# Three edits to a one-core, five-layer block: state-space coefficients loaded and computed first, step sizes cut in four, and a bias table copied 16 times instead of 128

## What is computed

```python
# first block: an input projection, a causal convolution, softplus step sizes, a chunked scan
h = rms_norm(x, norm_g[l]);  proj = h @ w_in[l]
xbc = jax.nn.silu(causal_dwconv(xbc, ssd_conv_w[l], ssd_conv_b[l]))
dt = jax.nn.softplus((dt_raw + ssd_dt_bias[l]).astype(jnp.float32))
y = ssd_scan(xs, dt, -jnp.exp(ssd_a_log[l]), bs, cs)
# second block, layer 0 (s5_mixer): coefficients from parameters alone
dt = jnp.exp(log_dt)[:, None];  mag = jnp.exp(lr * dt)
ab_re, ab_im = mag * jnp.cos(li * dt), mag * jnp.sin(li * dt)
den = lr * lr + li * li;  nr = ab_re - 1.0
f_re = (nr * lr + ab_im * li) / den;  f_im = (ab_im * lr - nr * li) / den
# second block, layer 1 (sliding_window_attention): a bias by distance, added to the scores
dist = qi + WINDOW - kj
bias = rel_bias[t5_bucket(jnp.maximum(dist, 0))]
s = jnp.where(valid, s + bias, NEG_INF)
```

## Time and profile before

| | us |
|---|---|
| median of three runs | 2254.06 (2251.0 to 2259.76) |
| the profiled execution's own time | 2256.19 |
| its span | 2254.4 |
| TensorE busy | 2045.3 (91%) |
| VectorE busy | 1289.9 (57%) |
| ScalarE busy | 872.2 (39%) |
| GpSimd busy | 477.9 (21%) |
| mean granted TensorE clock | 0.959 |

### The profile page before, as it was taken

How to read it: one execution, slowest core, us unless ns; L and a number is a source line. 1 busy time by engine, 2 the same in 40 slices (tenths; PEclk the granted TensorE clock), 3 DMA queues, 4 the chain that set the end, 5 groups by cost and what they waited for, 6 DMA issues and landing times.

```text
span 2254.4 us, 25022 instructions
## 1 busy us (share of the span) xinstructions
PE 2045.3 (91%) x10070; PEld 1593.4 (71%) x10070; DVE 1289.9 (57%) x1830; ACT 872.2 (39%) x1263; POOL 477.9 (21%) x386
## 2 busy tenths in 40 slices
PE   6897999999999999999998888999889989889986
PEld 4685676678747887868787766777767755567865
DVE  6985666643728436455446532666376466647384
ACT  4223555522149313432233343335542344444232
POOL 1854222141437614024300100001001010100001
PEclk9998999999999999999999999999999999999998
DMA  3241111123422525524546627211122210123211
GB/s 135 83 154 66 57 38 38 57 98 115 144 91 94 157 91 163 187 74 141 178 117 152 154 76 146 97 38 57 57 98 75 94 38 19 38 75 117 98 57 56
DMA packets 53138, 215.26 MB, mean 95 GB/s; under 512 B 6048, under 2 KB 23104, under 8 KB 32672
## 3 DMA queue, kind: packets, MB, share of 16 engines
q1 hardware_dynamic: 22896, 162.54, 20.7%
q0 software_dynamic: 9488, 35.94, 5.7%
q10 hardware_dynamic: 20640, 15.19, 3.1%
HBM read 196.14 MB, written 17.50 MB: 95 GB/s over the span
## 4 chain that ended last, share of the span: by engine, by line
PE 61%; DVE 11%; ACT 5%; issue 3%; DMA 2%; ACTq 1%; POOL 0%; DVEq 0%
PE bank L482 17%; PE bank L483 17%; PE bank L484 17%; PE bank L481 2%; DVE ring_low L444 1%; ACT ring_high L439 1%; PE bank L3133 1%; ACT swa_s L3037 1%; PE bank L3160 1%; DMA ring<-slabs 1%; ACTq L2405 1%; PE bank L1930 1%; DVE swa_s L2974 1%; DVE lru_x L1844 1%; DVE gated_low L2832 1%
## 5 line engine op out<-in xcount | busy, mean ns | idle before, releaser
L482 PE MATMUL bank<-h_high,ring_high 128*128 128x512 f32 x1248 | 505.2, 405 | 46.3 <-DVE h_low L1356 22.4
L444 DVE TENSOR_TENSOR ring_low<-ring,ring_high 128x2048 fp32r<-128x2048 f32 x136 | 329.9, 2427 | 339.7 <-ACT ring_high L439 339.5
L483 PE MATMUL bank<-h_low,ring_high 128*128 128x512 f32 x1248 | 493.1, 395 | 0.0
L484 PE MATMUL bank<-h_high,ring_low 128*128 128x512 f32 x1248 | 492.3, 394 | 0.0
L439 ACT ACTIVATE ring_high<-ring 128x2048 fp32r<-128x2048 f32 x145 | 277.4, 1913 | 510.5 <-PE bank L484 494.1
L482 PEld LDWEIGHTS bank<-h_high,ring_high 128*128 128x128 f32 x1248 | 239.0, 192 | 120.4 <-issue 59.4
L483 PEld LDWEIGHTS bank<-h_low,ring_high 128*128 128x128 f32 x1248 | 239.0, 192 | 52.3 <-issue 3.9
L484 PEld LDWEIGHTS bank<-h_high,ring_low 128*128 128x128 f32 x1248 | 238.6, 191 | 51.2
L482 PE MATMUL bank<-gated_high,ring_high 128*128 128x512 f32 x256 | 106.2, 415 | 25.6 <-issue 18.6
L444 POOL TENSOR_TENSOR ring_low<-ring,ring_high 128x2048 fp32r<-128x2048 f32 x9 | 43.3, 4807 | 366.4 <-ACT ring_high L439 366.4
L483 PE MATMUL bank<-gated_low,ring_high 128*128 128x512 f32 x256 | 103.7, 405 | 0.0
(11 more groups left out here) (518 smaller groups left out, 3963.7 us busy)
## 6 DMA issues: line engine op xcount, KB each, us to landing
ring<-slabs SPq DMA_DIRECT2D x149, 1024.0 KB, 4.9
s_outputs<-s_ca POOLq DMA_DIRECT2D x4, 1152.0 KB, 6.8
x<-xT SPq DMA_DIRECT2D x2, 2048.0 KB, 8.8
s_b<-s_br POOLq DMA_DIRECT2D x8, 512.0 KB, 4.4
s_rows<-s_powers POOLq DMA_DIRECT2D x16, 256.0 KB, 6.7
s_inputs<-s_w POOLq DMA_DIRECT2D x8, 512.0 KB, 3.1
s_ck<-s_outputs POOLq DMA_DIRECT2D x1, 4096.0 KB, 23.7
s_wv<-s_inputs ACTq DMA_DIRECT2D x8, 512.0 KB, 4.1
```

The lines of the kernel that those rows point to most:

```text
L444: dve.tensor_tensor(self.ring_low[:, s % RING, :], self.ring[:, s % RING, :], self.ring_high[:, self.splits_before[s] % AHEAD, :].bitcast( ...
L482: pe.matmul(out, w[0], x[0], start=start, stop=False)
L483: pe.matmul(out, w[0], x[1], start=False, stop=False)
L484: return pe.matmul(out, w[1], x[0], start=False, stop=stop)
```

## The change

Three edits. **First**, `stage_load` splits the one load of `cols` in three on ScalarE's queue: the 96 columns of the s5 parameters first, then what is ahead of them, then what is behind. Both halves of `s5_coefficients` move from the middle of `stage_xbc` to `stage_load`: on ScalarE ahead of the square root and of the wait for x, on VectorE ahead of the wait for the other columns. **Second**, the step sizes' VectorE work is cut: three operations behind tile 4, six behind tile 8, three behind tile 12, and the last one together with the sums behind tile 16. ScalarE's `split_high` of tile i+1 now stands before the SiLU of tile i. **Third**, the bias rows are written 16 times each instead of 128 times (384 KB), and the table is read back with eight transfers of 16 partitions each.

```diff
@@ stage_load
-            act.dma_start(C.cols[:], io["cols"]).then_inc(cols.sem, 16)
+            act.dma_start(C.cols[:, own], io["cols"][:, own]).then_inc(s5_cols.sem, 16)
+            act.dma_start(C.cols[:, 0:a], io["cols"][:, 0:a]).then_inc(cols.sem, 16)
+            act.dma_start(C.cols[:, a + 96:NCOL], io["cols"][:, a + 96:NCOL]).then_inc(cols.sem, 16)
+            act.wait_ge(s5_cols.sem, s5_cols.base + 16)
+            s5_act(act)
             act.wait_ge(C.consts.sem, C.consts.at(0))
             act.activation(C.eps8[:, 6:7], C.eps[:], ACT.Sqrt)
             act.wait_ge(loaded.sem, loaded.base + 16)
...
-            dve.wait_ge(cols.sem, cols.base + 16)
+            dve.wait_ge(s5_cols.sem, s5_cols.base + 16)
+            s5_dve(dve)
+            dve.wait_ge(cols.sem, cols.base + 32)
@@ stage_xbc, vector
-            s5_dve(dve)
...
-            def step_sizes():
-                dve.wait_ge(dts.sem, dts.at(1))
-                log1p_small(C, dve, L.S1[:], L.S2[:], L.S3[:], L.S4[:])
-
             def step_sums():
+                log1p_end(C, dve, L.S1[:], L.S2[:], L.S4[:])
...
                 if i == 4:
-                    step_sizes()
-                if i == 9:
+                    dve.wait_ge(dts.sem, dts.at(1))
+                    log1p_ratio(C, dve, L.S1[:], L.S2[:])
+                if i == 8:
+                    log1p_terms(C, dve, L.S2[:], L.S3[:], L.S4[:], 15, 9)
+                if i == 12:
+                    log1p_terms(C, dve, L.S2[:], L.S3[:], L.S4[:], 7, 3)
+                if i == 16:
                     step_sums()
@@ stage_xbc, scalar
-            s5_act(act)
...
-                if i >= 3:
-                    C.split_high(act, u)
+                if 3 <= i + 1 < len(tiles):
+                    C.split_high(act, tiles[i + 1][0])
@@ swa_bias, gpsimd
-        pool.dma_start(scr, L.BV[:].unsqueeze(1).to_broadcast([16, P, 384])).then_inc(s.sem, 16)
+        pool.dma_start(scr, L.BV[:].unsqueeze(1).to_broadcast([16, 16, 384])).then_inc(s.sem, 16)
         pool.wait_ge(s.sem, s.base + 16)
-
-        skewed = bass.AP(tensor=scr.tensor, offset=127, ap=[[383, P], [P * 384, 16], [1, 256]])
-        pool.dma_start(L.BT[:], skewed).then_inc(s.sem, 16)
+        for a in range(8):
+            skewed = bass.AP(tensor=scr.tensor, offset=127 - 16 * a, ap=[[383, 16], [16 * 384, 16], [1, 256]])
+            pool.dma_start(L.BT[16 * a:16 * a + 16], skewed).then_inc(s.sem, 16)
```

More of the change, by code:

```diff
@@ L505, in stage_load @@
     nc, io = C.nc, C.io
-    loaded, cols = C.reserve("loaded", 16), C.reserve("cols_loaded", 16)
+    loaded, cols, s5_cols = C.reserve("loaded", 16), C.reserve("cols_loaded", 32), C.reserve("s5_cols_loaded", 16)
+    s5_act, s5_dve = s5_coefficients(C)
+    a = COL_AT["lam_re"]
+    own = slice(a, a + 96)
     made = C.made = C.reserve("made", 4)
@@ L664, in conv_tile, with log1p_ratio @@
             C.vchain.link(dve, ins)
-def log1p_small(C, dve, e, s, s2, acc):
+def log1p_ratio(C, dve, e, s):
     ln = C.vchain.link
@@ L672, in log1p_small, with log1p_terms, log1p_end @@
     ln(dve, dve.tensor_tensor(s, s, e, ALU.mult))
-    ln(dve, dve.tensor_tensor(s2, s, s, ALU.mult))
-    ln(dve, dve.tensor_scalar(acc, s2, 2.0 / 17, None, ALU.mult))
-    for k in range(15, 1, -2):
-        ln(dve, dve.scalar_tensor_tensor(out=acc, in0=acc, scalar=2.0 / k, in1=s2, op0=ALU.add, op1=ALU.mult))
-    ln(dve, dve.scalar_tensor_tensor(out=e, in0=acc, scalar=2.0, in1=s, op0=ALU.add, op1=ALU.mult))
+def log1p_terms(C, dve, s, s2, acc, first, last):
+    ln = C.vchain.link
+    if first == 15:
+        ln(dve, dve.tensor_tensor(s2, s, s, ALU.mult))
+        ln(dve, dve.tensor_scalar(acc, s2, 2.0 / 17, None, ALU.mult))
+    for k in range(first, last - 1, -2):
+        ln(dve, dve.scalar_tensor_tensor(out=acc, in0=acc, scalar=2.0 / k, in1=s2, op0=ALU.add, op1=ALU.mult))
+def log1p_end(C, dve, e, s, acc):
+    C.vchain.link(dve, dve.scalar_tensor_tensor(out=e, in0=acc, scalar=2.0, in1=s, op0=ALU.add, op1=ALU.mult))
+def log1p_small(C, dve, e, s, s2, acc):
+    log1p_ratio(C, dve, e, s)
+    log1p_terms(C, dve, s, s2, acc, 15, 3)
+    log1p_end(C, dve, e, s, acc)
 def stage_xbc(C, L, items, norm):
@@ L692, in stage_xbc @@
     tiles = [(u, None) for u in us[1:]] + [C.take_tile(KD) for _ in range(21)]
-    s5_act, s5_dve = s5_coefficients(C)
     tables = Tables(C, L, items)
@@ L2863, in swa_bias @@
     u = C.take_given(7)
-    s = C.reserve("swab", 16 * 2)
+    s = C.reserve("swab", 16 * 9)
     ld = C.reserve("swa_loaded", 16 * 3)
@@ L3001, in evac_z @@
                 times_root(dve, j, C.bank[u.b]).then_inc(C.bank_read[u.b], 1)
-            dve.wait_ge(L.bias_laid.sem, L.bias_laid.base + 32)
+            dve.wait_ge(L.bias_laid.sem, L.bias_laid.base + 16 * 9)
             for b in range(2):
@@ L3476, in build @@
     io["s5_conv"] = scratch("s5_kernels", [NB5, P, 240])
-    io["bias_rows"] = nc.dram_tensor("bias_rows", [16, P, 384], F32, kind="Internal").ap()
+    io["bias_rows"] = nc.dram_tensor("bias_rows", [16, 16, 384], F32, kind="Internal").ap()
     C = Core(nc, io)
```

## The result

The changed kernel takes 2242.02 us (median of 4 runs, 2239.32 to 2243.32), the kernel before 2254.82 (the three runs known and a fourth, 2251.0 to 2259.76). The ratio is 0.994, with a 95% interval of 0.9918 to 0.9962: 13 us faster, a little over a half per cent. The forecast was 2238, its range 2227 to 2248, so the total lies inside. Its parts do not all. The profiled execution took 2243.32 us with a span of 2241.4, against 2256.19 and 2254.4 before, so the two spans, 13.0 us apart, may stand for the medians.

What follows compares the result with a forecast made beforehand. TensorE, busy 91% of the span, was taken to bound the kernel, with VectorE's sum of work setting the convolution stage's end. Gains 7.7 + 10.9 + 7.7 less 9.9 gave 16.4 us, so 2238 us, range 2227 to 2248.

Steps and rivals of the forecast that it cites:

- coefficients at the start: Head, before the norm: the coefficient chain delays squares and additions; loss 9.9 us (bounds 8.0 and 13.4).
- convolution stage: From the full bank on: 123.8 us instead of 131.5, gain 7.7 us (bounds 2 and 11).
- wait for the tables: Behind the convolution stage: GpSimd's tables end earlier and the wait goes whole; gain 10.9 us (bounds 9.5 and 11.2).
- bias rows: End of the state-space layer: smaller write, late slab in time; gain 7.7 us (bounds 6.0 and 7.7).
- 1.5 us for GpSimd beside the norm: Head: GpSimd working beside the norm's additions lengthens them by 1.5 us, bounds nothing and 5 us.
- The slower rival: GpSimd beside the norm: head loses 16.5 us more, the stage's low parts 12; 2265 us, chance 0.04.
- the early landing: Head: first piece of `cols` lands by 3.9 us, loss 3.4 instead of 9.9; 2231.5 us, chance 0.12.
- 19.5 in all: Convolution stage: VectorE's four step-size pieces priced at 4.4, 4.0, 2.1 and 8.8 us.
- The sign for the second rival: Convolution stage still taking over 129 us from the full bank would prove the second rival.
- the second rival: Convolution stage: VectorE's sum of work is unchanged, pieces only move TensorE's stalls; gain 2 us, 2244 us, chance 0.2.
- the third rival: The slower rival: GpSimd lengthens VectorE's norm operations and the stage's low parts; 2265 us, chance 0.04.

Runs made afterwards that it cites:

- edit 3 alone: Kernel before with only the bias-row edit (16 copies of each row, eight reads); 2246.82 us, ratio 0.9953.
- edit 2 alone: Kernel before with only the step sizes cut in four and ScalarE's high parts one tile earlier; 2250.29 us, ratio 0.9983.

## Why the prediction was right or wrong

**The total was right, in good part by luck.** Against the forecast of 16.4 us stand 13.0 of span. The stage missed by 10.6 us; what the tables gave above the forecast, and scatter elsewhere, made up for over half of it. Term by term:

| term | forecast | measured |
|---|---|---|
| coefficients at the start | -9.9 (bounds 8.0 and 13.4) | -9.5, to the marker at 49.01 and 58.52 |
| convolution stage | +7.7 (bounds 2 and 11) | -2.9, from there to the last tile |
| wait for the tables | +10.9 | +12.5, to the scan's first decay |
| behind it, the clock | none | +1.6, to the second decay |
| bias rows | +7.7 | +8.0 |
| elsewhere (217 to 1338 us, and from 1413) | none | +1.8 and +1.5 |

The last row may be no more than scatter between executions: with edit 3 alone, where nothing is changed between 219 and 1370 us, the profiled execution gains 3.4 + 0.7 = 4.1 us on the one before in that stretch.

**The head was right, with its mechanism.** The first piece went one for one with x's packets (55 and 54 of the two queues from 4 to 6 us) and landed at 8.8 us, as said. The rival in which its 8 rows pass in x's first round, by 3.9 us, did not come. It was the rule of the Trainium skill, "DMA: Bandwidth & Descriptors", section "Queues, rings and completion order", by which an engine drains a whole packet of some 9 to 17 descriptors before it switches; the trace disagrees for this queue. The chain behind it was 1.3 us shorter than my 9.4: I counted ScalarE's first table load, and it ran at 2.21 while the data were on their way. Of the 1.5 us for GpSimd beside the norm, 1.3 came: 16.6 us from first addition to restart instead of 15.3. The slower rival, 16.5 more there, did not. What the sum lacked is the clock: 1.2 us for the longer stretch at 1.2 GHz behind the longer norm. The price of the early landing, 6.5 us, had dropped the 1.5 for GpSimd and is 5.0 with it; the run with the columns first, where they landed at 3.2 us, measured 5.65.

**The stage was wrong, and the step that failed is the one that priced the pieces**: "19.5 in all" for the four pieces, and 4.3 us for each tile, from durations of the kernel before. I moved work to other times and GpSimd's chain 32 us earlier, and kept the lengths that both had had with the old neighbours. The 11.4 us of the series were mostly taken (7.2 us) while GpSimd waited for a transfer; I had not looked at GpSimd's row beside them. I had also misread where the stage begins. The bank that is full at 49.0 is that of the last of the four opening tiles, the marker above; the first of the four was full at 46.9 (TensorE's 87th matmul behind the restart, of 96). The coefficients held VectorE up for 3.1 us there, not 1.1. They cost 1.0 all the same, since the low part behind them needs a high part that ScalarE ends at 50.93: that this number fits is luck. From the marker the stage takes 134.4 us (58.52 to 192.95) instead of the 123.8 forecast, 10.6 more: 7.2 by the pieces (26.7, counted as the 19.5 were), 1.8 by the low parts, and 2.0 by waits of VectorE for TensorE that stayed, which is 0.4 too much in sum. A TensorE wait of 5.7 us for a low part stood where I had said none over 3. The sign for the second rival, over 129 us, came true, and its time of 2244 is nearer than mine. But its cause, that the same sum of work bites, is refuted by the run with the tables held back: the sum itself grew. With edit 2 alone, where GpSimd's chain stayed in its place, the stage did gain 7.7 us and the pieces did take 19.6 in all, though not piece by piece: the sum held beside the old neighbours and not beside the new ones that edit 1 brought.

**Half of the lock was priced.** The Trainium skill, "SBUF — State Buffer", section "Who interferes with whom", says that VectorE and GpSimd take the port pair they share for a whole instruction. The traces agree with the page: operations that read the banks (three in 2.32 us) never changed, those with operands in SBUF went from 0.41 to 2.37 (`TENSOR_SCALAR`), 0.68 to 3.06 (`TENSOR_TENSOR`), and GpSimd's from 2.27 to 4.3. In the sum I applied this lock to GpSimd's chain alone, where 15 us of slack made it harmless. VectorE's chain, which had none, was the other side of the same lock; only the third rival, with a chance of 0.04, put a price on it.

**The tables were right in their mechanism, and worth more than I said.** ScalarE's first exponential gained 10.8 us for the 10.9 forecast, but I took the wrong one of two counts: the scan's first decay hangs on VectorE, and VectorE gained 12.4 and not the 11.2 of its wait, because two operations ahead of it (1.17 and 1.46 us beside GpSimd's work) now take 0.29 each and wait 0.9 more. The sum also ended too soon: the clock that comes back between the two decays was worth 1.6. I had read the same effect in the earlier trace rows and not used it here.

**The bias rows were right**: 7.2 us alone and 8.0 in place, at the upper bound of 7.7, and the write landed in 5.5 us for the 6 forecast. A wait of ScalarE for a slab is still there, 0.94 us at 1395.8, and it costs TensorE nothing. The eight reads took 13.2 us at the median, and nobody waited for them.

**The range** held, since the bounds of the stage were wide, though not wide enough on its side: it had a gain as its lower end. Nothing in the rows excluded a loss.

## What to carry to other kernels

A duration from a trace belongs to its neighbours: when VectorE work with SBUF operands moves, or GpSimd work moves beneath it, read GpSimd's row at the new place first, and price an operation at up to its own time and that of the GpSimd instruction beside it (0.68 us became 3.06 beside one of 2.59 and one of 2.75). GpSimd's waits for its own transfers are the places for such pieces; here moving them there was worth 7.5 us of the stage and some 6 of the total (2235.64 against 2242.02; 2231.4 against 2236.86 with the columns first, measured side by side), by medians whose intervals overlap. A small transfer that somebody waits for goes ahead of the large one; here that was done on the same queue, and a start later for the large one alone was not tried.

## What the runs showed that I had not expected

- Two engines that hold each other up lengthen each other's instructions: GpSimd's of 2.27 us took up to 4.3 beside VectorE's. But a chain with transfers in it can shift by more than that for another reason: with the step sizes spread, GpSimd's ended 5.9 us earlier at the same start, 4.8 of them in its transfers.
- A table load of ScalarE is done ahead while the engine waits for a transfer (at 2.21 us, with the data there at 8.8), so it costs nothing behind such a wait.
- 48 KB on the queue beside x's landed in 8.0 us, ahead of x on its own queue in 2.4; the main piece of `cols`, alone on the other queue then and ahead of x too, took 2.6 us instead of 10.6.
